# Post-norm projections of the second model's layers computed with tokens on the partitions

## The chip, the cores and the metric

The kernel runs on one core of one Trainium2 chip. The metric is the device time of one execution in microseconds (us), the median over runs. Three runs of the kernel before gave 1899.44, 1899.73 and 1900.01 us.

## What is computed

Two small models, one behind the other, on 256 tokens of width 1024, in float32, with two layers each. The first has three residual steps per layer (feed-forward, a mixer of attentions, feed-forward) and norms only before each step. The second has a mixer and a feed-forward per layer, and norms on both sides of each:

```python
    merged = gates[:, :, 0] * y_a + gates[:, :, 1] * y_b + gates[:, :, 2] * y_c
    x = x + rms_norm_2(merged @ w_o, n_post_mix)
    h = rms_norm_2(x, n_pre_ffn)
    gu = h @ w_ffn_gu
    ffn = (jax.nn.silu(gu[..., :D_FF_2]) * gu[..., D_FF_2:]) @ w_ffn_down
    return x + rms_norm_2(ffn, n_post_ffn)
```

The change is about the closing norms, `n_post_mix` and `n_post_ffn`: a projection (`w_o` or `w_ffn_down`), the mean square of its result per token, the root, the gain, the sum into the residual, and the start of the next step, which reads it.

## The kernel before, in words

The program is a list of ten stages (`STAGES`, built by `program_parts`, L167): f1, mix, f2 twice, then mix2, ff2, mix2, ff2, numbered 0 to 9. Every weight matrix is cut into parts of at most 2048 columns per partition. The parts pass through a ring of three buffers: SyncE (SP) loads part i into `raw`, ScalarE (ACT) rounds it into `w_hi` (`split_hi`, L324), VectorE (DVE) puts the rest into `w_lo` (`split_lo`, L333), and TensorE (PE) multiplies with both. `split_hi(i)` waits until part i-3 has been used (`part_used`), and each engine does its instructions in the order in which they are written. Activations are split in the same way, into `x_hl` (high and low), and a product is three matrix products: high by high, high by low, low by high.

The residual `h` lies with channels on the partitions: eight chunks of 128 channels by 256 tokens. In the feed-forward (`ffn`, L651 on PE) the weights are the stationary operand, and a row of 512 moving columns is high and low of one chunk for all 256 tokens. In the mixer the activations are stationary, one token tile of 128 tokens at a time, and the weights move.

The closing norms of stages 6, 7 and 8, which the change touches, go like this before it. The projection leaves channels on the partitions, so that a sum over channels runs across partitions. ACT squares each chunk and multiplies it by the gain (`post_gain`, L1237), DVE adds the squares up (`add_square`, L1703), PE sums over partitions with a column of ones (`closing_sum`, L593), DVE takes the mean (L1733 or L1735), GpSimd (POOL) the root (L2343), PE spreads the root over all partitions (`to_rows`, L609), DVE multiplies eight chunks by it (L1744) and adds them to `h` (L1750), ACT makes the high part of the next stage's input (L1232) and DVE the low part (L1700). Products of the next stage start as soon as the first chunk is there, and its first two parts are gone through chunk by chunk (L531/L532 in a feed-forward, `project_by_chunk`, L753, in a mixer). During the norm PE does 16 products of zeros (`warm_up`, L579).

Stage 9, the last, already has its down projection with tokens on the partitions (`down_rows`, L621 on PE; `row_square`, L1249 on ACT; `last_rows`, L1781 on DVE): hidden activations stationary, weights moving in rows of 512, one accumulator bank per token tile and half of the channels. There the sum over channels is the accumulator that comes with ACT's square.

Of the kernel before, what the change touches and what calls it, by code (L numbers as in the profile page):

```python
# [8 lines left out]
F32 = mybir.dt.float32  # L9
# [157 lines left out]
def program_parts():  # L167
# [28 lines left out]
H_BEFORE = [KC * r - 3 * sum(t == "mix2" for t, _, _ in STAGES[:r]) + 3 * sum(t == "ff2" for t, _, _ in STAGES[:r]) for r in range(len(STAGES))]  # L196

CHUNKWISE = [s > 0 and STAGES[s - 1][0] in ("mix2", "ff2") for s in range(len(STAGES))]
CHUNKS = [sum({"mix": 7, "mix2": 6}.get(t, 4) for t, _, _ in STAGES[:s]) for s in range(len(STAGES))]
SQUARES = [KC + KC * s + KC * POSTS_BEFORE[s] for s in range(len(STAGES))]  # L200
# [13 lines left out]
def build(nc, w, out):  # L214

    with ExitStack() as ctx:
# [61 lines left out]
        gained_ready, sets_clear = sem("gained_ready"), sem("sets_clear")  # L278
# [62 lines left out]
        def wait_chunk(engine, s, c):  # L341
# [7 lines left out]
            elif tag == "mix2":  # L349
                if c % 4 == 3:  # L350
                    engine.wait_ge(part_used, i0 + len(MIX2) + 2 + c // 4 + 1)
                else:
                    engine.wait_ge(chunk_done, CHUNKS[s] + 3 * (c // 4) + c % 4 + 1)
# [12 lines left out]
        def down_row_bank(m, t):  # L366
            return (6, 2)[m] + t
# [20 lines left out]
        gained = region(11264, (KC, SEQ))  # L388
        squares = rows.rearrange("p t (c n) -> p (t c) n", n=SEQ)
# [183 lines left out]
        def _(pe):  # L573
# [19 lines left out]
            def closing_sum(bank, s):  # L593

                pe.wait_ge(acc_ready, due("acc_ready"))
                for t in range(TT):
                    nc.tensor.matmul(ps[:, bank, t:t + 1], acc[:, t * P:(t + 1) * P], ones_col[:, 0:1], start=t == 0,
                                     stop=False, skip_group_check=True)
                warm_up(1)
                pe.wait_ge(sq_ready, SQUARES[s] + KC)  # L600
                for t in range(TT):
                    m = nc.tensor.matmul(ps[:, bank, t:t + 1], squares[:, KC - 1, t * P:(t + 1) * P], ones_col[:, 0:1], start=False,
                                         stop=True, skip_group_check=True)
                m.then_inc(sum_done, 1)
# [16 lines left out]
            def down_rows(i0, h0):  # L621
# [4 lines left out]
                def products(x, t):  # L626
# [4 lines left out]
                    for k in range(kc):  # L631
                        a = (hid_hl[:, k0 + k, v, t * P:(t + 1) * P] for v in range(2))
                        mm = matmul3(ps[:, down_row_bank(m, t), :], *a, hi[:, k, :], lo[:, k, :], k0 + k == 0, k0 + k == FF - 1)
                    return mm

                pe.wait_ge(hrows_ready, 4)
# [9 lines left out]
                for t in range(TT):  # L646
                    for x in (len(k_parts) - 2, len(k_parts) - 1):
                        mm = products(x, t)
                    mm.then_inc(token_done, 1)

            def ffn(s, i0, post_norm):  # L651
                x0 = due("xlo_ready", KC) - KC
                u0 = due("up_free", 2 * STEPS) - 2 * STEPS
                h0 = due("hidlo_ready", STEPS) - STEPS
                stats_at = 1 if i0 and not CHUNKWISE[s] else 2
                if CHUNKWISE[s]:
                    part_ready(i0 + 1)
                    for c in range(KC):
                        pe.wait_ge(xlo_ready, x0 + c + 1)
                        for p in range(2):  # L660
                            hi, lo = view(w_hi, i0 + p), view(w_lo, i0 + p)
                            for f in range(2):
# [1800 lines left out]
```

## Time and profile before

| | |
|---|---|
| median of three runs | 1899.73 us |
| the profiled execution's own time | 1899.96 us |
| its span, first to last instruction | 1897.8 us |
| PE busy | 1884.5 us (99%) |
| PE weight loads busy | 1639.1 us (86%) |
| DVE busy | 1340.7 us (71%) |
| ACT busy | 967.5 us (51%) |
| mean granted PE clock | 0.998 of full |
| DMA | 172 GB/s over the span |

Busy times are of instructions and overlap: a PE that streams, and one that does zeros, are both busy. So the page tells which engine bounds the kernel, and the timeline must tell what the time between two stages consists of. Matmuls overlap too: what one costs in a stream is the distance between two starts, not the length printed.

### The profile page before, as it was taken

The page shows a single profiled execution, that of the slowest core. Times are in us where ns is not written, and L with a number is a line of the kernel's source. Part 1 is how long each engine was busy: PE and PEld are TensorE (multiplying, and loading weights), DVE is VectorE, ACT ScalarE, POOL GpSimd, SP SyncE. Part 2 cuts the span into 40 slices and gives each one's busy share as a digit, 9 for nine tenths or more (in the row PEclk, how much of TensorE's full clock was granted, in tenths as well). Part 3 has the DMA queues.
Part 4 walks back from the last instruction along what each step waited for, and adds up shares of the span by engine and source line. Part 5 has one row for each costly group of instructions (what it writes and reads, how often), then busy time and mean ns, then how long its engine had stood idle before and what let it go on. Part 6 is the DMA issues. An engine that isn't in the chain of part 4 may idle for free.

```text
span 1897.8 us, 26159 instructions
## 1 busy us (share of the span) xinstructions
PE 1884.5 (99%) x10937; PEld 1639.1 (86%) x10940; DVE 1340.7 (71%) x1485; ACT 967.5 (51%) x1216; POOL 161.5 (9%) x158
## 2 busy tenths in 40 slices
PE   9999999999999999999999999999999999999998
PEld 7888879888888888898888888888888888888887
DVE  7877687787687777868776555569765654568764
ACT  5444656544444446665434665455444665455442
POOL 0000522100000006121000200000000110000000
PEclk9999999999999999999999999999999999999999
DMA  7554543455555555334554443445545343445452
GB/s 289 205 185 177 189 153 104 150 200 184 187 196 186 189 182 178 134 112 178 192 190 167 165 171 133 164 169 189 188 173 187 136 174 135 158 178 180 186 176 112
DMA packets 47491, 327.28 MB, mean 172 GB/s; under 512 B 5520, under 2 KB 5520, under 8 KB 11536
## 3 DMA queue, kind: packets, MB, share of 16 engines
q1 hardware_dynamic: 46512, 323.25, 47.0%
q10 hardware_dynamic: 864, 2.38, 0.3%
q8 instruction: 86, 1.41, 0.3%
q14 instruction: 29, 0.24, 0.0%
HBM read 324.56 MB, written 1.05 MB: 172 GB/s over the span
## 4 chain that ended last, share of the span: by engine, by line
PE 97%; DVE 1%; ACT 1%; issue 0%; DMA 0%; POOL 0%; DVEq 0%; POOLq 0%; ACTq 0%
PE ps L537 34%; PE ps L544 18%; PE ps L525 10%; PE ps L527 10%; PE ps L526 10%; PE ps L865 2%; PE ps L531 1%; PE ps L831 1%; PE ps L820 1%; PE ps L822 1%; PE ps L821 1%; PE ps L854 1%; PE ps L582 1%; PE ps L532 1%; PE ps L741 1%
## 5 line engine op out<-in xcount | busy, mean ns | idle before, releaser
L331 ACT CAST w_hi<-raw 128x2048 fp32r<-128x2048 f32 (+4 forms) x314 | 580.1, 1849 | 574.0 <-PE ps L527 193.7
L338 DVE TENSOR_TENSOR w_lo<-raw,w_hi 128x2048 fp32r<-128x2048 f32 (+4 forms) x314 | 700.1, 2231 | 237.8 <-ACT w_hi L331 235.1
L537 PE MATMUL ps<-x_hl,w_hi 128*128 128x512 f32 x1968 | 459.3, 390 | 0.0
L537 PEld LDWEIGHTS ps<-x_hl,w_hi 128*128 128x128 f32 x1968 | 365.2, 188 | 73.2
L525 PE MATMUL ps<-w_hi,x_hl 128*128 128x512 f32 (+3 forms) x672 | 262.5, 391 | 0.0
L527 PE MATMUL ps<-w_hi,x_hl 128*128 128x512 f32 (+3 forms) x672 | 254.3, 378 | 0.0
L526 PE MATMUL ps<-w_lo,x_hl 128*128 128x512 f32 (+3 forms) x672 | 253.6, 377 | 0.0
L544 PEld LDWEIGHTS ps<-x_hl,w_lo 128*128 128x128 f32 x1968 | 243.6, 192 | 5.5 <-DVE w_lo L338 1.4
L544 PE MATMUL ps<-x_hl,w_lo 128*128 128x256 f32 x1968 | 246.8, 283 | 0.8 <-DVE w_lo L338 0.8
L1816 DVE TENSOR_REDUCE ffn_tmp<-ps 128x512 f32<-128x1024 f32 x132 | 161.2, 1223 | 100.3 <-PE ps L544 50.2
L537 PE MATMUL ps<-hid_hl,w_hi 128*128 128x512 f32 x836 | 196.4, 390 | 0.0
L537 PEld LDWEIGHTS ps<-hid_hl,w_hi 128*128 128x128 f32 x836 | 154.9, 188 | 30.8
L2343 POOL TENSOR_TENSOR stat<-stat,const 128x2 f32<-128x2 f32 (+1 forms) x15 | 25.3, 1686 | 1441.4 <-DVE stat L1717 816.5
L525 PEld LDWEIGHTS ps<-w_hi,x_hl 128*128 128x128 f32 x672 | 126.5, 188 | 23.4 <-issue 2.8
L527 PEld LDWEIGHTS ps<-w_hi,x_hl 128*128 128x128 f32 x672 | 126.3, 188 | 23.6
L526 PEld LDWEIGHTS ps<-w_lo,x_hl 128*128 128x128 f32 x672 | 126.7, 189 | 19.9
L544 PEld LDWEIGHTS ps<-hid_hl,w_lo 128*128 128x128 f32 x836 | 105.2, 191 | 2.9
L544 PE MATMUL ps<-hid_hl,w_lo 128*128 128x256 f32 x836 | 106.1, 283 | 0.0
L1232 ACT ACTIVATE x_hl<-h,gains 128x256 fp32r<-128x256 f32 x80 | 39.0, 506 | 94.5 <-DVE h L1899 81.7
L1273 ACT ACTIVATE ffn_tmp<-ffn_tmp 128x512 f32<-128x512 f32 x66 | 41.8, 633 | 72.8 <-DVE ffn_tmp L1822 72.5
L1276 ACT CAST hid_hl<-ffn_tmp 128x512 fp32r<-128x512 f32 x66 | 41.1, 622 | 26.9 <-DVE ffn_tmp L1827 25.9
L531 PE MATMUL ps<-x_hl,w_hi 128*128 128x512 f32 x144 | 51.7, 402 | 0.0
(288 smaller groups left out, 2204.3 us busy)
## 6 DMA issues: line engine op xcount, KB each, us to landing
raw<-in_parts SPq DMA_DIRECT2D x278, 1024.0 KB, 4.8
raw<-in_parts SPq DMA_DIRECT2D x20, 768.0 KB, 4.2
raw<-in_parts SPq DMA_DIRECT2D x4, 928.0 KB, 4.5
raw<-in_parts SPq DMA_DIRECT2D x4, 864.0 KB, 4.4
raw<-in_parts SPq DMA_DIRECT2D x6, 512.0 KB, 3.7
raw<-in_parts SPq DMA_DIRECT2D x4, 576.0 KB, 3.6
const<-in_const ACTq DMA_DIRECT2D x1, 1093.0 KB, 5.1
h<-in_x_t SPq DMA_DIRECT2D x1, 1024.0 KB, 7.6
```

The source lines that it names most:

```text
L331: nc.scalar.copy(w_hi[:, i % RING, 0:n_of(i)], raw[:, i % RING, 0:n_of(i)]).then_inc(high_ready, 1)
L338: nc.vector.tensor_tensor(w_lo[:, s, 0:n], raw[:, s, 0:n], w_hi[:, s, 0:n].bitcast(F32), ALU.subtract).then_inc(low_ready, 1)
L525: nc.tensor.matmul(out_, a_hi, b_hi, start=start, stop=False, skip_group_check=True)
L526: nc.tensor.matmul(out_, a_hi, b_lo, start=False, stop=False, skip_group_check=True)
L527: return nc.tensor.matmul(out_, a_lo, b_hi, start=False, stop=stop, skip_group_check=True)
L531: nc.tensor.matmul(ps[:, bank, :], w_h, hl.rearrange("p x n -> p (x n)"), start=start, stop=False, skip_group_check=True)
L537: m = nc.tensor.matmul(ps[:, bank, :], w_h(c), hl(c).rearrange("p x n -> p (x n)"), start=start and c == 0, stop=stop and c == kc - 1, ski ...
L544: m = nc.tensor.matmul(ps[:, bank, 0:SEQ], w_l(c), hl(c)[:, 0, :], start=start and c == 0, stop=stop and c == kc - 1, skip_group_check=True)
L1232: nc.scalar.activation(x_hi(c), h[:, c, :], ACT.Copy, scale=gains[:, s, c:c + 1]).then_inc(xhi_ready, 1)
L1273: nc.scalar.activation(g_tmp, g_tmp, ACT.Silu).then_inc(silu_ready, 1)
L1276: nc.scalar.copy(hid_hl[:, p - 1:p + 1, 0, :], u_tmp.rearrange("p (f n) -> p f n", f=2)).then_inc(hidhi_ready, 1)
L1816: return nc.vector.tensor_reduce(dst.rearrange("p (f n) -> p f n", f=2), ps[:, b:b + 2, :].rearrange("p b (x n) -> p b n x", x=2), AX_X, A ...
```

## The change

The closing projections of stages 6, 7 and 8 get tokens on the partitions, as in stage 9. For the down projection of stage 7 that also changes how its weights are cut (`ffn_parts(..., True)`): twelve parts either way. `closing_sum`, `post_gain`, `after_post`, `post_norm` and `project_by_chunk` go away. The products of the first token tile (t0) are brought to an end before those of the second (t1), and t0's norm, with `scale_rows` on ACT, PE's transposes back (`rows_turn`) and the sums into `h` (`add_rows` on DVE), stands among t1's products. `h` and `x_hl` are then written in halves of 128 tokens by instructions of 128 by 128.

The core of the diff:

```diff
-        parts += ffn_parts("w_ffn_gu_2", 0, "w_ffn_gu_2", F, "w_ffn_down_2", l, l == DEPTH - 1)
+        parts += ffn_parts("w_ffn_gu_2", 0, "w_ffn_gu_2", F, "w_ffn_down_2", l, True)
...
+            def rows_turn(t, m, used=False):
+                pe.wait_ge(rows_scaled, due("rows_scaled"))
+                for c in range(4 * m, 4 * m + 4):
+                    tr = nc.tensor.transpose(ps[:, 2 * t + m, (c % 4) * P:(c % 4 + 1) * P], y_rows[:, t, c * P:(c + 1) * P], ident)
+                    if used and c == 4 * m:
+                        tr.then_inc(part_used, 1)
+                tr.then_inc(rows_turned, 1)
...
                 for t in range(TT):
-                    for x in (len(k_parts) - 2, len(k_parts) - 1):
-                        mm = products(x, t)
-                    mm.then_inc(token_done, 1)
+                    products(len(k_parts) - 2, t)
+                    if t == 1 and s < LAST:
+                        rows_turn(0, 0, True)
+                    products(len(k_parts) - 1, t).then_inc(token_done, 1)
+                if s < LAST:
+                    rows_turn(0, 1, True)
...
+                    if FROM_ROWS[s] and m == 0:
+                        rows_turn(1, 0)
+                        rows_turn(1, 1)
...
-                project_out(k, WO2, 3, read=(gained_ready, KC * POSTS_BEFORE[s]), x=merged_x)
-                closing_sum(STATS_MIX, s)
-                warm_up(5)
-                pe.wait_ge(gained_ready, KC * POSTS_BEFORE[s] + KC)
-                pe.wait_ge(root_ready, due("root_ready"))
-                to_rows(POST_ROW, post)
-                warm_up(10)
...
+                out_rows_of(2, 0, range(4), 11).then_inc(token_done, 1)
+                part_ready(k + 3)
+                out_rows_of(3, 0, range(4)).then_inc(token_done, 1)
+                out_rows_of(2, 1, range(4)).then_inc(token_done, 1)
+                rows_turn(0, 0, True)
+                out_rows_of(3, 1, range(2))
+                rows_turn(0, 1)
+                out_rows_of(3, 1, range(2, 4)).then_inc(token_done, 1)
+                warm_up(8, row_bank(s, 0, 0))
+                rows_turn(1, 0, True)
+                rows_turn(1, 1)
```

On ACT (feed-forward, then mixer) and on DVE (`add_rows`):

```diff
+                    split_hi(act, after)
+                    row_done()
+                    row_square(s, 1, 0)
+                    scale_rows(s, 0)
+                    for c in range(4):
+                        if c == 2:
+                            row_done()
+                            row_square(s, 1, 1)
+                        next_x_half(s + 1, 0, c, h0 + c + 1)
+                    split_hi(act, after + 1)
+                    scale_rows(s, 1)
+                    for c in range(4):
+                        next_x_half(s + 1, 1, c, h0 + KC + c + 1)
+                    for t in range(TT):
+                        for c in range(4, KC):
+                            next_x_half(s + 1, t, c, h0 + KC * t + c + 1)
+                    for c in range(KC):
+                        square(h[:, c, :], c)
+                    split_hi(act, after + 2)
...
+                for c in range(KC):
+                    if c == 5:
+                        row_done()
+                        row_square(s, 1, 1)
+                    next_x_half(s + 1, 0, c, h0 + c + 1)
+                scale_rows(s, 1)
...
+                for c in range(4 * m, 4 * m + 4):
+                    nc.vector.scalar_tensor_tensor(h[:, c, half], ps[:, 2 * t + m, (c % 4) * P:(c % 4 + 1) * P], gains[:, POST_GAIN[s], c:c + 1],
+                                                   h[:, c, half], ALU.mult, ALU.add).then_inc(h_ready, 1)
```

How the instructions move, at three places.

**PE, from the last products of `w_o` to the first of the feed-forward, before.** L820 to L822 are the products, L597 and L602 the sum over partitions, L609 the spreading, L582 the zeros.

```order
L822 MATMUL ps<-y_hl,w_lo 128x256
L597 MATMUL ps<-const,arena 128x1 x2
L582 MATMUL ps<-unsel 128x512
L602 MATMUL ps<-const,rows 128x1 x2
L582 MATMUL ps<-unsel 128x512 x5
L609 MATMUL ps<-const,stat 128x128 x2
L582 MATMUL ps<-unsel 128x512 x10
L531 MATMUL ps<-x_hl,w_hi 128x512
```

**The same place now.** L528 to L530 are the products with rows of 512, L600 the transposes, L585 the zeros.

```order
L530 MATMUL ps<-w_hi,y_hl 128x512
L600 MATMUL ps<-const,arena 128x128 [waits rows_scaled]
L600 MATMUL ps<-const,arena 128x128 x3
...
L530 MATMUL ps<-w_hi,y_hl 128x512
L585 MATMUL ps<-unsel 128x512 x8
L600 MATMUL ps<-const,arena 128x128 [waits rows_scaled]
L600 MATMUL ps<-const,arena 128x128 x3
L600 MATMUL ps<-const,arena 128x128 [waits rows_scaled]
L600 MATMUL ps<-const,arena 128x128 x3
L534 MATMUL ps<-x_hl,w_hi 128x512 [waits xlo_ready,low_ready]
```

Half of the sixteen transposes stand among the products, half behind the zeros; all zeros come before the first transpose of t1.

**DVE at the same place now.** L1763 is `add_rows`, L1770 the low half of the next input, L1754 (`row_root`) t1's mean square.

```order
L1763 SCALAR_TENSOR_TENSOR h<-ps,gains,h 128x128 x3
L1770 SCALAR_TENSOR_TENSOR x_hl<-h,gains,x_hl 128x128 [waits xhi_ready] x4
L1754 SCALAR_TENSOR_TENSOR stat<-stat 128x1 [waits outsq_ready]
L1763 SCALAR_TENSOR_TENSOR h<-ps,gains,h 128x128 [waits rows_turned]
```

t1's mean square stands behind the last low halves of t0.

**ACT, from stage 7 to the mixer of stage 8, before.** L1238 is the gain, L331 a part's rounding, L1232 the next input, L1235 a square of `h`.

```order
L1238 ACTIVATE arena<-ps,gains 128x256 x2
L331 CAST w_hi<-raw 128x1728 [waits part_used,raw_in1]
L1232 ACTIVATE x_hl<-h,gains 128x256 [waits h_ready] x2
L1235 ACTIVATE rows<-h 128x256 x2
```

**The same place now.**

```order
L1240 ACTIVATE x_hl<-h,gains 128x128 [waits h_ready] x2
L338 CAST w_hi<-raw 128x2048 [waits part_used,raw_in0]
L1246 ACTIVATE arena<-ps,stat 128x512 [waits root_ready]
L1246 ACTIVATE arena<-ps,stat 128x512
L1240 ACTIVATE x_hl<-h,gains 128x128 [waits h_ready] x12
L1234 ACTIVATE rows<-h 128x256 x8
L338 CAST w_hi<-raw 128x1728 [waits part_used,raw_in1]
```

The rounding of the next stage's second part has moved behind t0's first inputs, and that of its third part (1728 columns) behind all inputs and squares.

## Rows read from the trace of the kernel before

**Rows 1.** The chain that ended last, shares of the span by engine.

```profile
PE 97%; DVE 1%; ACT 1%; issue 0%; DMA 0%; POOL 0%; DVEq 0%; POOLq 0%; ACTq 0%
```

**Rows 2.** Stretch around stages 6 and 7: from:to, us, busy (count) by engine, PEclk, DMA, GB/s.

```profile
1260.00:1280.00 20.00, 19.50 (x143) 16.90 (x144) 10.73 (x18) 12.81 (x23) 0.70 (x1) 1.00 0.44 159
```

**Rows 3.** Timeline of PE, w_o into stage 7: start us, length us, instruction, shape, count.

```profile
1248.63 0.28 PE L820 MATMUL ps<-x_hl,w_hi 128*128 128x256 f32 x1
...
1251.51 1.04 PE L741 MATMUL ps<-const,rows 128*128 128x128 f32 x8
1252.30 0.36 PE L820 MATMUL ps<-x_hl,w_hi 128*128 128x256 f32 x1
...
1272.41 0.28 PE L822 MATMUL ps<-y_hl,w_lo 128*128 128x256 f32 x1
...
1275.90 2.32 PE L582 MATMUL ps<-unsel 128*128 128x512 bf16 x10
1278.19 0.47 PE L531 MATMUL ps<-x_hl,w_hi 128*128 128x512 f32 x1
...
1289.74 3.85 PE L537 MATMUL ps<-x_hl,w_hi 128*128 128x512 f32 x16
```

**Rows 4.** Timeline of stage 9: a product of 512 columns, then t0's square, accumulator and root.

```profile
1887.54 0.39 PE L526 MATMUL ps<-w_lo,hid_hl 128*128 128x512 f32 x1
1887.77 0.39 PE L527 MATMUL ps<-w_hi,hid_hl 128*128 128x512 f32 x1
...
1888.19 0.60 ACT L1251 ACTIVATE arena<-ps 128x512 f32<-128x512 f32 x1 [8.42 <-PE ps L527]
1888.69 0.19 ACT L1251 ACTIVATION_READ_ACCUMULATOR arena<-ps 128x1 f32 x1
...
1889.15 0.55 POOL L2343 TENSOR_TENSOR stat<-stat,const 128x1 f32<-128x1 f32 x1 [162.98 <-DVE stat L1797]
```

**Rows 5.** Groups by form, ACT and DVE: shapes, count, busy us, mean ns, idle before.

```profile
L331 ACT CAST w_hi<-raw 128x2048 fp32r<-128x2048 f32 x276 | 526.2, 1907 | 509.0 <-PE ps L527 177.5 <-PE ps L544 161.8 <-PE ps L537 130.3
L1232 ACT ACTIVATE x_hl<-h,gains 128x256 fp32r<-128x256 f32 x80 | 39.0, 506 | 94.5 <-DVE h L1899 81.7 <-DVE h L1750 12.1
L1235 ACT ACTIVATE rows<-h 128x256 f32<-128x256 f32 x80 | 30.2, 402 | 0.0
L1284 ACT ACTIVATE neg_ident<-const 128x128 bf16<-128x128 f32 x1 | 0.3, 294 | 0.0
L1700 DVE SCALAR_TENSOR_TENSOR x_hl<-h,gains,x_hl 128x256 fp32r<-128x256 f32 x80 | 39.6, 511 | 10.4 <-ACT x_hl L1232 10.4
L338 DVE TENSOR_TENSOR w_lo<-raw,w_hi 128x1728 fp32r<-128x1728 f32 x4 | 7.8, 1952 | 0.0
L2158 DVE SCALAR_TENSOR_TENSOR arena<-arena,ps 128x128 f32<-128x128 f32 x8 | 2.4, 345 | 0.1
```

**Rows 6.** Timeline, stage 7's down projection into the mixer of stage 8.

```profile
1401.92 1.30 PE L537 MATMUL ps<-hid_hl,w_hi 128*128 128x512 f32 x5
...
1463.47 0.28 PE L527 MATMUL ps<-hid_hl,w_lo 128*128 128x256 f32 x1
...
1464.79 1.64 ACT L331 CAST w_hi<-raw 128x1728 fp32r<-128x1728 f32 x1
...
1468.70 0.47 PE L525 MATMUL ps<-w_hi,x_hl 128*128 128x512 f32 x1
...
1483.28 0.70 POOL L2343 TENSOR_TENSOR stat<-stat,const 128x2 f32<-128x2 f32 x1 [17.48 <-DVE stat L1717]
1484.07 1.27 ACT L1518 ACTIVATE arena<-ps,stat 128x512 f32<-128x512 f32 x2 [6.30 <-POOL stat L2343]
1485.39 0.87 PE L741 MATMUL ps<-const,arena 128*128 128x128 f32 x6
```

**Rows 7.** The start of the kernel: ten products of zeros after a gap, and the granted clock.

```profile
7.21 4.01 PE L582 MATMUL ps<-unsel 128*128 128x512 bf16 x10 [2.11 <-ACT w_hi L315]
...
7.50:8.00 0.50, 0.50 (x3) 0.14 (x2) 0.50 (x2) 0.50 (x2) 0.00 (x0) 0.69 1.02 426
...
11.00:11.50 0.50, 0.50 (x4) 0.43 (x3) 0.50 (x2) 0.50 (x2) 0.00 (x0) 0.90 1.08 459
```

More of the change, by code:

```diff
@@ L195, with half_place @@
 POSTS_BEFORE = [sum(t in ("mix2", "ff2") for t, _, _ in STAGES[:r]) for r in range(len(STAGES))]
[L196 to L200, printed above, removed]
+H_BEFORE = [KC * r for r in range(len(STAGES))]
+FROM_ROWS = [s > 0 and STAGES[s - 1][0] in ("mix2", "ff2") for s in range(len(STAGES))]
+CHUNKS = [sum({"mix": 7, "mix2": 0, "ff2": 0}.get(t, 4) for t, _, _ in STAGES[:s]) for s in range(len(STAGES))]
+SQUARES = [KC + KC * s for s in range(len(STAGES))]
+def half_place(s, t, c):
+    if STAGES[s - 1][0] == "mix2":
+        return KC * t + c + 1
+    return KC * (c // 4) + 4 * t + c % 4 + 1
 class Due:
@@ L780, in project @@
                                 pe.wait_ge(*ready(o + c))
+                            if t == 1 and c0 == 0 and late is not None:
+                                pe.wait_ge(*late(o + c))
                             a_hi, a_lo = x(o + c)
@@ L803, in project_out @@
                 hi, lo = view(w_hi, i), view(w_lo, i)
-                last = m == 3 or parts is WO2 and m == 2
+                last = m == 3
                 for n in range(n_all // P):
@@ L1169, in mixer2 @@
                 for m, (name, _, _, k, kc, g, last) in enumerate(MIX2):
-                    free = ready = None
+                    free = ready = late = None
                     if g >= 2 and k == 0:
@@ L1185, in mixer2 @@
                         x, ready = whole_x, lambda c: (S["tlo_ready"], 8 + c // 2)
[L1186 to L1189 removed]
+                    project(i0 + m, pair_bank(g), kc, o, k == 0, last, free, ready, x, lambda: within_part(m), late)
                     after_part(m)
@@ new lines, in mixer2 @@
+                part_ready(k + 3)
[8 more added lines that the diff above has]
+                rows_turn(1, 1)
+                for t in range(TT):
+                    due("root_ready")
@@ L1766, in post_norm, with next_x_lo_half, sum_squares @@
+            def next_x_lo_half(s, t, m):
+                half = slice(t * P, (t + 1) * P)
+                for c in range(4 * m, 4 * m + 4):
+                    dve.wait_ge(xhi_ready, due("xhi_ready"))
+                    nc.vector.scalar_tensor_tensor(x_lo(c)[:, half], h[:, c, half], gains[:, s, c:c + 1], x_hi(c)[:, half].bitcast(F32), ALU.mult,
+                                                   ALU.subtract).then_inc(xlo_ready, 1)
+            def sum_squares():
                 for c in range(KC):
@@ L1795, in last_rows @@
[L1795 to L1804 removed]
+                            row_mean(s, t, t + 1, True)
@@ new lines, in down_in_rows @@
+                            if s == LAST:
+                                gain_rows(0, t)
+                if s == LAST:
+                    for t in range(TT):
+                        row_root(s, t, TT + t + 1)
+                        step(gain_rows(1, t))
+                        dve.wait_ge(root_ready, due("root_ready", 0))
+                        for m in range(2):
+                            r = out_rows[:, t, 512 * m:512 * m + 512]
+                            nc.vector.scalar_tensor_tensor(r, r, post[:, t:t + 1], h_rows[:, t, 512 * m:512 * m + 512], ALU.mult,
+                                                           ALU.add).then_inc(out_ready, 1)
+                    return
@@ L1852, in ffn @@
                 scaled_gate(0)
-                if s and not CHUNKWISE[s]:
+                if s and not FROM_ROWS[s]:
                     split_lo(dve, i0 + 4)
```

342 lines of the change are left out of this document (141 added, 201 removed).

## The prediction

> **What bounds the kernel now.** I read the chain of waits first: 97% of it is PE [rows 1]. So time changes only where PE streams fewer columns, or where it has nothing useful to stream. The windows are all but full there too: PE is busy 19.50 of 20 us around the end of stage 6, at the full clock [rows 2]. That hides what the timeline shows: the last product of `w_o` starts at 1272.41, the first of stage 7 at 1278.19, and between them PE does sums, spreading and products of zeros [rows 3]. Products of 256 columns follow each other by 0.12 us, so the gap is 1278.19 - 1272.53 = 5.66 us. From stage 7 to 8 it is 1468.70 - 1463.59 = 5.11 [rows 6]. Stage 8 to 9 repeats the first. These three gaps, 16.4 us, and the form of the products are what the change can reach. The groups by form and stage 9, which already works by token tiles, give the prices [rows 4, 5].
>
> **Products.** Rows of 512 columns follow each other by 0.227 us [rows 4]; two of 256 cost 0.24. `w_o` now has 8 x 8 x 3 = 192 products of 256: 23.04 us. By rows it has 2 x 2 x 8 x 3 = 96 of 512: 21.8. That saves 1.27 us, twice. Stage 7's down projection takes 1463.59 - 1401.92 = 61.67 [rows 6] and becomes 22 x 2 x 2 x 3 = 264 of 512: 59.85. That saves 1.8.
>
> **Transposes.** Each closing adds 16, eight of them among products. The trace has eight in 1252.30 - 1251.51 = 0.79 us [rows 3], 0.10 each, so 0.8 us of PE time beside the 0.8 in the gap, three times. The Trainium skill, "TensorE: Matmul & The Clock Gate", Part 4: PE-mode transpose, has about 275 ns for one in a kernel's context; if all 48 queued at that, they would take 13.2 us instead of 4.8, and the row speaks against it: that is one's length, and they overlap.
>
> **Small instructions.** `h`, the high and the low parts go from 256 to 128 columns each. DVE: a scalar_tensor_tensor of 128 columns takes 0.345 us, one of 256 takes 0.511 [rows 5]. Starts of like instructions lie some 0.08 to 0.1 closer than their length, so I take 0.27 apart. The ends are 0.22 (half a step of 256) and 0.38 (nearly what 256 costs); I stay at the row of the same shape. ACT: a rounding with the gain takes 0.506 for 256 columns, a copy of 128 takes 0.294 [rows 5]. I take 0.40 long and 0.30 apart, ends as for DVE. A rule speaks against smaller pieces: the Trainium skill, "VectorE: DVE Perf Modes", The TRN2 errata, says each instruction pays a fixed latency whatever its size and wants tiles of 512 or more; its formula gives ScalarE 352 cycles, 0.29 us, for 128 columns, which would leave the sum below as it is. The trace agrees so far: half the columns cost well over half the time.
>
> **w_o into a feed-forward, twice.** t0 first. Its square, accumulator, mean and root take 1.7 us from its last product's slot (1888.00 to 1889.70 in stage 9 [rows 4]), the first scaling 0.7 more: ready at 2.5, wanted by PE at 2.72 (12 products of t1). So t0's norm hides, with 0.2 to spare. Then t1, in us from the end of its last product:
> - result seen and square with accumulator: 0.2 + 0.7 = 0.9;
> - DVE isn't free: the mean square stands behind t0's last low halves, whose high halves of chunks 5 to 7 stand behind this square on ACT (each 0.30): 2.1;
> - mean 0.16, hand-over 0.08, root 0.55: 2.9;
> - scaling 0.69, then four transposes with their drain, 0.57: 4.3;
> - four sums into `h` by DVE at 0.27 before its first low half: 5.4; the low half 0.35: 5.8.
>
> The gap is 5.8 us instead of 5.66: the norm is one tile instead of two but has more steps in line. After it, the first part is fed by pairs of 0.7 us a chunk, slower than DVE's 0.54 (a sum and a low part), so it doesn't stall. The second part's rounding (1.9 us on ACT [rows 5]) ends 1.4 us before PE wants it. In all, from the first product of `w_o` to the end of the second part: before, 1289.74 - 1248.63 = 41.11 [rows 3]. Then: products 21.8, transposes within it 0.8 + 0.8, gap 5.8, two parts of 5.6: 40.2. **-0.9 us, twice.** With DVE and ACT at their ends -1.4 or +1.2 each.
>
> **Stage 7 into the mixer.** Here only t0 is needed to start. t1's last product ends at 0. PE turns t0's second half (0.4), and the four chunks of t0 that are ready cover 2.7. t1: DVE's mean square comes only after four low halves and four sums of t0, at 3.0; root at 3.7, scaling seen at 4.4. PE has been idle from 3.1 to 4.4, turns t1 (1.0), and waits until 6.5 for the first low half. t1's first chunks last until 9.3. DVE then splits the second part (2.2) before t0's upper half, 0.6 lost; eight chunk steps of 0.68 end at 15.3. Now the third part. ACT rounds it behind the last high half (12.1), eight squares of 0.31 (14.6; 0.402 long [rows 5]) and its own 1.64 [rows 6]: 16.2. DVE's 1.9 [rows 5] gives 18.2. **PE stands 2.9 us there**, where before ACT rounded that part at 1464.79, before the inputs [rows 6]. Then the sum of squares: as before, PE waits behind that part for root and scaling to turn the mixer's first rows (1483.28, 1484.07, 1485.39 [rows 6]), but these follow DVE's split of the fourth part: some 1.6 us of waiting instead of 0.3. The turn starts 24.8 us after t1's end. From the start of the down projection: 59.85 + 0.4 (one turn among the products) + 24.8 = 85.1; before, 1485.39 - 1401.92 = 83.5 [rows 6]. **+1.6 us**, ends +0.8 and +4.1. Behind that both do the same.
>
> **Sum of the work**: 2 x (-0.9) + 1.6 = -0.2; with the ends -2.0 and +6.5.
>
> **The clock.** Before, zeros fill every gap. Now PE has holes: behind eight zeros (1.7 us) idle 1.95, transposes, idle 1.1; in stage 8 idle 1.3, transposes, idle 1.1, and the 2.9. The one hole in the trace is 2.1 us, before the second set of zeros at the start; half a us later the clock fell to half (0.69 in that half us) and was full again within 11.00 to 11.50 (0.90 [rows 7]). Ten products of zeros then took 4.01 instead of 2.32 [rows 3]: 1.7 us for one fall. Part of a fall lies in waiting, so I take 1.1 to 1.7 for a fall in front of a feed-forward and less before the mixer. It need not happen: the transposes divide the holes. I take two falls in three: **+2.0 us**, ends 0 and +5.
>
> **Forecast.** -0.2 + 2.0 = +1.8 on the profiled execution's 1899.96 (span 1897.8 and 2.2 around it): 1901.8; the median of the runs stands 0.2 lower, so **1901.6 us**. A change of less than 0.2%, 3.8 us, is about what a measurement of this kernel can't tell from none.
>
> **Rivals.**
> - *The clock holds.* For it: transposes keep the array at work, and zeros come just before. Against: rows 7. Only the sum remains: -0.2, 1899.5. Chance 0.23.
> - *Small instructions at their upper end, slower by over 0.2%.* Where DVE and ACT take 0.38 per half, the gap before a feed-forward is 7.6 instead of 5.8 and the mixer's third part comes 2.4 later. t0's scaling also runs late among t1's products (0.2 us to spare), and each such wait delays t1 as well. Sum +6.5, with longer holes and so a fall almost surely, +1.5: 1907.7. It decides from about 0.33 on. For it: four engines hand over ten times in line. Against: the row of 0.345 [rows 5]. Chance 0.20.
> - *Faster.* The lower end (-2.0), the clock held, and DVE's wait behind t0's low halves gone because ACT has done them before t1's last product: that gives 1.2 back at each feed-forward: -4.4, 1895.3. For it: DVE is idle there otherwise. Against: chunk 5 is put behind the square by the order of the program. Chance 0.10.
> - *The change hides nothing*: t0's norm, as priced, ends as PE wants it; if it took 2 us more (ACT or DVE still in a part's splitting, 1.9 and 2.2 us), PE would stand among t1's products: 2 us at each closing on top of +1.8, 1907.5. Against: the last split before it ends over 1 us earlier. Chance 0.05.
>
> The forecast itself has the remaining 0.42; its own range is 1899.5 to 1904.
>
> **Numbers.** Of the forecast's chance a quarter (0.10) lies above 1903.5, as do the second and last rivals (0.20 and 0.05): slower 0.35. Faster by over 0.2% needs the third rival: 0.10. Within 0.2%: the rest of the forecast and the held clock, 0.55. The range from 1896.5 to 1906.5 leaves out 0.08 below and 0.12 above.
>
> **What would show it.** Right: 96 products by `w_o` at 0.227 apart; a gap of about 5.8 us before the feed-forwards, with DVE's mean square behind t0's last low halves; PE standing 1.1 to 1.5 us on both sides of t1's transposes; in stage 8 a wait of about 3 us for `w_lo` of the third part; stretches of half clock behind the holes. Wrong: half instructions at other prices than 0.27 and 0.30, a gap under 4 us, a third part that isn't waited for, or a clock of 1.00 in every stretch.

## The result, and the profile after

The changed kernel takes 1901.93 us in the median, against 1899.72 for the kernel before on the same chip: a ratio of 1.0013, interval 1.0007 to 1.0019. That is 2.2 us more, against 1.9 forecast. One of its twenty runs (7588.06 us), and one of the eleven of the first experiment below (3135.74), was disturbed: the medians given count them (without them they are 1901.13 and 1900.76), and the ratios, the counts of runs and the ranges leave them out. The profiled execution took 1900.76 us, its span is 1898.3.

The 19 runs do not lie evenly: ten between 1900.4 and 1901.1, at a mean granted clock of about 0.999, six between 1902.7 and 1903.7 at about 0.997, three between 1904.6 and 1905.5 at 0.995 to 0.996. No run lies between 1901.13 and 1902.74. So the median of 1901.93 is the middle of an empty stretch, where no run was; the nineteen have a median of 1901.13 (+1.4) and a mean of 1902.16 (+2.45 against the other kernel's mean of 1899.71). The kernel before spread over 1.3 us in all. So the change did two things: it moved the fastest group by +1.0 (its median is 1900.68), and it spread the runs.

Busy times from the page, then the stretch that answers to [rows 2] (from:to, us, busy by PE, PEld, DVE, ACT, POOL, PEclk, DMA, GB/s):

```profile
PE 1875.5 (99%) x10594; PEld 1620.3 (85%) x10596; DVE 1330.3 (70%) x1512; ACT 969.3 (51%) x1228; POOL 162.7 (9%) x161
...
PE 95%; DVE 2%; ACT 1%; DMA 0%; issue 0%; POOL 0%; DVEq 0%; POOLq 0%; SPq 0%; ACTq 0%
```

```profile
1260.00:1280.00 20.00, 17.22 (x86) 13.23 (x86) 11.09 (x37) 12.39 (x30) 1.10 (x2) 1.00 0.29 104
```

PE has lost 9 us of busy time, and the chain of waits now runs over DVE and ACT in 3% instead of 2%. In the stretch it is busy 17.22 instead of 19.50 us, at the full clock in this execution.

**In front of a feed-forward.** The timeline of PE, `w_o` of stage 6 into stage 7, answers to [rows 3]:

```profile
1248.06 0.39 PE L528 MATMUL ps<-w_hi,x_hl 128*128 128x512 f32 x1
...
1250.80 1.09 PE L725 MATMUL ps<-const,rows 128*128 128x128 f32 x8
...
1268.09 0.60 PE L600 MATMUL ps<-const,arena 128*128 128x128 f32 x4
...
1269.90 0.60 PE L600 MATMUL ps<-const,arena 128*128 128x128 f32 x4
...
1271.50 0.40 PE L530 MATMUL ps<-w_hi,y_hl 128*128 128x512 f32 x1
1271.96 1.67 PE L585 MATMUL ps<-unsel 128*128 128x512 bf16 x7
1275.36 1.24 PE L600 MATMUL ps<-const,arena 128*128 128x128 f32 x8 [1.72 <-ACT arena L1246]
1277.58 0.47 PE L534 MATMUL ps<-x_hl,w_hi 128*128 128x512 f32 x1 [0.99 <-DVE x_hl L1770]
...
1286.87 3.40 PE L547 MATMUL ps<-x_hl,w_lo 128*128 128x256 f32 x27
```

L600 are the transposes back, L585 the zeros (the trace has seven of the eight). Neither transpose of t0 carries a wait: its norm is hidden. From the last product's slot (1271.73) to the first of stage 7 is 5.85 us. The second part ends 16 low products of 0.12 behind 1286.87, at 1288.79: 40.73 us after the start of `w_o`. What DVE does in that gap:

```profile
1272.94 0.94 DVE L1770 SCALAR_TENSOR_TENSOR x_hl<-h,gains,x_hl 128x128 fp32r<-128x128 f32 x3 [0.56 <-ACT x_hl L1240]
1273.79 0.15 DVE L1754 SCALAR_TENSOR_TENSOR stat<-stat 128x1 f32<-128x1 f32 x1
1276.05 1.13 DVE L1763 SCALAR_TENSOR_TENSOR h<-ps,gains,h 128x128 f32<-128x128 f32 x4 [2.10 <-PE ps L600]
1277.09 1.13 DVE L1770 SCALAR_TENSOR_TENSOR x_hl<-h,gains,x_hl 128x128 fp32r<-128x128 f32 x4
```

The mean square of t1 (L1754) does stand behind t0's last three low halves, 2.06 us after the last product.

**Stage 7 into the mixer** answers to [rows 6]; ACT and DVE first, then PE:

```profile
1471.93 1.28 ACT L1240 ACTIVATE x_hl<-h,gains 128x128 fp32r<-128x128 f32 x4 [2.89 <-DVE h L1763]
1473.12 2.55 ACT L1234 ACTIVATE rows<-h 128x256 f32<-128x256 f32 x8
1475.58 3.15 ACT L338 CAST w_hi<-raw 128x1728 fp32r<-128x1728 f32 x2
...
1477.22 1.96 DVE L345 TENSOR_TENSOR w_lo<-raw,w_hi 128x1728 fp32r<-128x1728 f32 x1 [3.51 <-ACT w_hi L338]
```

```profile
1400.81 0.40 PE L528 MATMUL ps<-w_hi,hid_hl 128*128 128x512 f32 x1
...
1465.51 1.24 PE L600 MATMUL ps<-const,arena 128*128 128x128 f32 x8 [0.98 <-ACT arena L1246]
1467.64 0.50 PE L528 MATMUL ps<-w_hi,x_hl 128*128 128x512 f32 x1 [0.90 <-DVE x_hl L1770]
...
1479.24 0.47 PE L528 MATMUL ps<-w_hi,x_hl 128*128 128x432 f32 x1 [2.56 <-DVE w_lo L345]
...
1486.34 0.87 PE L725 MATMUL ps<-const,arena 128*128 128x128 f32 x6
```

PE stands 2.56 us for the third part's low half, whose rounding waits on ACT behind the squares, after ACT had been idle for 2.89 us. In this execution the clock falls behind that hole. Stretches with PE alone (from:to, us, busy, PEclk, DMA, GB/s):

```profile
1479.00:1480.00 1.00, 0.76 (x3) 0.87 0.00 0
1480.00:1482.00 2.00, 2.00 (x7) 0.50 0.93 246
1484.00:1486.00 2.00, 2.00 (x12) 1.00 0.70 217
```

Full clock until the product behind the hole, then half (0.50, the level of 1.2 GHz), full again by 1484.

Three stretches hold the change (us; "full clock": from a run without a fall there):

| | before | forecast | after |
|---|---|---|---|
| `w_o` to the second part's end, stage 6 to 7 | 41.11 | 40.2 | 40.73 |
| the same, stage 8 to 9 | 41.12 | 40.2 | 40.84 |
| stage 7's down projection to the turn of the mixer's rows | 83.47 | 85.1 | 85.53; 85.01 at full clock |

At the full clock that makes -0.38 - 0.28 + 1.54 = +0.9, close to the +1.0 of the fastest group. What lifts the mean of the nineteen by another 1.5 us (1902.16 against 1900.68) is the spread.

The two profiled executions lie only 0.8 us apart, though the three stretches as profiled (85.53) make +1.4. The difference comes from the kernel's start: the ten zeros of [rows 7], which took 4.01 us at a fallen clock, take 2.33 here, and `w_o` of stage 6 starts 0.57 us earlier, at 1248.06 instead of 1248.63. The change touches nothing there.

```profile
7.14 2.33 PE L585 MATMUL ps<-unsel 128*128 128x512 bf16 x10 [1.59 <-ACT w_hi L322]
```

### The profile page after: what moved, and what is told of

Same layout as the page of the kernel before. It is cut to its first block, busy times and chain, and to the rows that moved or that the text cites. A ratio compares the mean times of both kernels' runs of the same rounds, so it can differ in the third digit from the quotient of the medians.

```text
span 1898.3 us, 25490 instructions
## 1 busy us (share of the span) xinstructions
PE 1875.5 (99%) x10594; PEld 1620.3 (85%) x10596; DVE 1330.3 (70%) x1512; ACT 969.3 (51%) x1228; POOL 162.7 (9%) x161
## 4 chain that ended last, share of the span: by engine, by line
PE 95%; DVE 2%; ACT 1%; DMA 0%; issue 0%; POOL 0%; DVEq 0%; POOLq 0%; SPq 0%; ACTq 0%
PE ps L540 32%; PE ps L547 17%; PE ps L528 12%; PE ps L530 11%; PE ps L529 11%; PE ps L838 2%; PE ps L804 1%; PE ps L534 1%; PE ps L827 1%; DVE w_lo L345 1%; PE ps L725 1%; PE ps L793 1%; PE ps L795 1%; PE ps L794 1%; PE ps L535 1%; PE ps L854 0%
## 5 line engine op out<-in xcount | busy, mean ns | idle before, releaser
L540 PE MATMUL ps<-x_hl,w_hi 128*128 128x512 f32 x2000 | 466.6, 390 | 0.0
L528 PE MATMUL ps<-w_hi,x_hl 128*128 128x512 f32 (+3 forms) x704 | 275.9, 392 | 3.8 <-DVE w_lo L345 2.6
L530 PE MATMUL ps<-w_hi,x_hl 128*128 128x512 f32 (+3 forms) x704 | 267.4, 380 | 0.0
L529 PE MATMUL ps<-w_lo,x_hl 128*128 128x512 f32 (+3 forms) x704 | 266.7, 379 | 0.0
L540 PE MATMUL ps<-hid_hl,w_hi 128*128 128x512 f32 x704 | 165.5, 390 | 0.0
L528 PEld LDWEIGHTS ps<-w_hi,x_hl 128*128 128x128 f32 x704 | 133.0, 189 | 28.5 <-DVE w_lo L345 4.0
L530 PEld LDWEIGHTS ps<-w_hi,x_hl 128*128 128x128 f32 x704 | 132.8, 189 | 24.9
L540 PEld LDWEIGHTS ps<-hid_hl,w_hi 128*128 128x128 f32 x704 | 130.4, 188 | 25.9
L547 PEld LDWEIGHTS ps<-hid_hl,w_lo 128*128 128x128 f32 x704 | 88.7, 191 | 2.5
L547 PE MATMUL ps<-hid_hl,w_lo 128*128 128x256 f32 x704 | 89.5, 283 | 0.0
L528 PE MATMUL ps<-w_hi,hid_hl 128*128 128x512 f32 x176 | 68.6, 390 | 0.0
L529 PE MATMUL ps<-w_lo,hid_hl 128*128 128x512 f32 x176 | 68.5, 389 | 0.0
```

The costliest lines, as they stand in the source:

```text
L528: nc.tensor.matmul(out_, a_hi, b_hi, start=start, stop=False, skip_group_check=True)
L529: nc.tensor.matmul(out_, a_hi, b_lo, start=False, stop=False, skip_group_check=True)
L530: return nc.tensor.matmul(out_, a_lo, b_hi, start=False, stop=stop, skip_group_check=True)
L540: m = nc.tensor.matmul(ps[:, bank, :], w_h(c), hl(c).rearrange("p x n -> p (x n)"), start=start and c == 0, stop=stop and c == kc - 1, ski ...
L547: m = nc.tensor.matmul(ps[:, bank, 0:SEQ], w_l(c), hl(c)[:, 0, :], start=start and c == 0, stop=stop and c == kc - 1, skip_group_check=True)
```

## The experiments

A fall is a stretch in which the granted clock drops from full to half. My theory: +0.9 us of work and waits, which is -0.7 in front of the feed-forwards and +1.5 in PE's wait for the mixer's third part; and on top of it falls of the clock in the holes in front of the feed-forwards, which come in some runs and make the groups. The rivals: the spread has another cause; the small instructions are the cost; t0's norm hides nothing.

### Zeros in the holes, all of them and by place

```diff
-                warm_up(8, row_bank(s, 0, 0))
+                warm_up(16, row_bank(s, 0, 0))
                 rows_turn(1, 0, True)
                 rows_turn(1, 1)
+                warm_up(5, row_bank(s, 0, 0))
...
                     if FROM_ROWS[s] and m == 0:
+                        warm_up(4, 6)
                         rows_turn(1, 0)
                         rows_turn(1, 1)
+                        warm_up(4, 6)
...
+                    if FROM_ROWS[s] and m == 2:
+                        warm_up(12, 6)
```

The first run has both pieces, the second only the upper one (in front of the feed-forwards), the third only the lower one (stage 8).

> The changed kernel, with products of zeros put into the holes that PE has in the three closings: eight more behind t1's last product and five more behind its transposes in front of the two feed-forwards, eight around t1's transposes and twelve before the third part at the start of stage 8. If falls of the clock in these holes are what makes many runs of the changed kernel longer by steps of some 2.3 us, then all runs lie near the fastest group, 1900.4 to 1901.2, the median falls from 1901.9 to about 1900.7, the profile shows no stretch of half clock at 1479.7 to 1483.1, and the runs' mean granted clocks are all alike. If the steps come from something else (transfers, the start of the kernel), the groups stay and the median stays at 1901.9 or more. If the length of the chain of small instructions is the cost, the zeros change nothing, or, where they last longer than the hole, add up to 0.5 us each.

> Only the zeros in front of the two feed-forwards. If the falls that come and go between runs lie in front of the feed-forwards (the profiled run has none there, but one in stage 8 in full), the groups at 1902.7 to 1905.5 disappear and the median is 1900.6 to 1901.2; the fall at 1480 in stage 8 stays. If they lie in stage 8, or at the kernel's start, the groups stay and the median is 1901.9.

> Only the zeros at the start of stage 8, around t1's transposes and before the third part. If the clock's fall at 1479.7 to 1483.1 costs time, the turn of the mixer's first rows comes earlier than 1486.3; at most by what of the fall does not lie in waiting, 0 to 1 us, since these rows wait for the chain over DVE, GpSimd and ScalarE. The groups of runs stay if the falls in front of the feed-forwards make them. If all falls are here, the groups go with this one alone.

Measured: 1900.82, 1900.96 and 1902.79 us. With zeros in front of the feed-forwards all runs, ten and eleven, lie between 1900.3 and 1901.5: the groups are gone. With zeros in stage 8 alone they stay: five runs at 1900.2 to 1901.0, five at 1902.8 to 1904.0, one at 1905.5. So the spread comes from the holes in front of the feed-forwards. The fall in stage 8 costs 0.5 us up to the turn in the changed kernel's profile (85.53 against 85.01 us with zeros there, where PE waits 1.17 us in front of the turn instead of not at all); 1900.82 against 1900.96 us is too close to show it.

One part of the second expectation missed: I had the fall at 1480 stay, and in that run's profile it isn't there. The clock fell one hole earlier, behind t1's transposes (columns of [rows 2]):

```profile
1468.00:1470.00 2.00, 1.86 (x4) 1.49 (x5) 2.00 (x5) 1.53 (x6) 0.00 (x0) 0.50 0.00 0
1480.00:1482.00 2.00, 2.00 (x12) 1.91 (x11) 1.93 (x4) 0.00 (x0) 0.00 (x0) 1.00 0.64 160
```

PE then waits 1.66 us for the third part instead of 2.56, and the turn comes at 85.01 us all the same: there the wait takes the whole fall, and it costs nothing. The profiles without zeros and with the mean square first, further down, show the same (waits of 1.64 and 1.63 us, turns at 85.00).

The profiled execution of the third run (1902.97 us) has a fall at both places in front of the feed-forwards. Its stretches with PE alone:

```profile
1278.00:1280.00 2.00, 2.00 (x8) 0.50 0.00 0
1709.00:1710.00 1.00, 1.00 (x5) 0.50 0.00 0
```

From the first product of a feed-forward to the end of its first part: 7.25 and 6.95 us, against 5.62 and 5.72 in the changed kernel's profile; 1.6 and 1.2 us for the two, together about the distance between this run's first two groups (medians 1900.34 and 1903.07, 2.7 us). They came together here. What decides in which run they come stays open.

### No zeros

```diff
-                warm_up(8, row_bank(s, 0, 0))
```

> The eight products of zeros before t1's transposes are taken out of the two closings in front of feed-forwards, so that the hole on their left grows from 1.7 to 3.4 us. If holes bring the clock down, each of the two falls comes in nearly every run: the profile shows a half-clock stretch behind both gaps, and the median rises by 2 to 4.6 us, to 1904 to 1906.5. If the clock does not mind holes of this length, nothing changes: 1901.9.

Measured: 1905.59 us, all seven runs between 1903.9 and 1905.9. Stretches behind the first closing, with the columns of [rows 2]:

```profile
1272.00:1275.00 3.00, 0.07 (x1) 0.00 (x0) 1.54 (x7) 1.77 (x6) 0.55 (x1) 1.00 0.01 3
1275.00:1276.00 1.00, 0.47 (x2) 0.48 (x3) 0.00 (x0) 1.00 (x2) 0.00 (x0) 0.72 0.00 0
1276.00:1282.00 6.00, 5.28 (x20) 4.34 (x19) 4.26 (x16) 4.18 (x10) 0.00 (x0) 0.50 0.00 0
```

Without zeros the clock is at half already during the transposes, for over 6 us. No run lies near the fastest group, so I take it that the falls came every time; only one of the seven has its trace. The eight products of zeros that the change has there turn a loss of some 4.9 us (1905.59 against 1900.68) in all runs into one of 2.3 to 4.6 in nine of nineteen.

### The third part rounded early

```diff
                         for c in range(4, KC):
                             next_x_half(s + 1, t, c, h0 + KC * t + c + 1)
+                        if t == 0:
+                            split_hi(act, after + 2)
                     for c in range(KC):
                         square(h[:, c, :], c)
-                    split_hi(act, after + 2)
```

> In stage 7's closing ScalarE rounds the mixer's third part before t1's upper high halves and the eight squares, in an idle stretch of 2.9 us, instead of behind them. If my step on the third part is right (PE stands 2.7 us for its low part, and the mixer's rows wait behind that), PE does not stand there, and the turn of the mixer's first rows comes 2 to 4 us earlier than 85.5 us after the start of the down projection; the kernel gets 2 to 4 us faster than the changed one, 1898 to 1899.5 in the median. If the turn is held by the sum of squares and the root instead, the stall only moves and the time stays within 0.7 us of 1901.9.

Measured: 1897.52 us, half a us under the range that I expected, with seven of eleven runs at 1897.0 to 1897.8 (the others, up to 1901.9, at the lower clocks of the falls). The timeline of ACT, then of PE:

```profile
1469.06 1.63 ACT L338 CAST w_hi<-raw 128x1728 fp32r<-128x1728 f32 x1
1472.03 1.28 ACT L1240 ACTIVATE x_hl<-h,gains 128x128 fp32r<-128x128 f32 x4 [1.34 <-DVE h L1764]
1473.22 2.55 ACT L1234 ACTIVATE rows<-h 128x256 f32<-128x256 f32 x8
```

```profile
1482.63 0.87 PE L725 MATMUL ps<-const,arena 128*128 128x128 f32 x6 [0.71 <-ACT arena L1529]
```

The rounding fits into the idle stretch, PE does not stand for the third part, and the turn comes 81.71 us after the start of the down projection instead of 85.01 at the full clock: -3.3 us, and 1.8 less than in the kernel before. So the +1.5 hung on this one place in ACT's order.

### The mean square first

```diff
                 add_rows(s, 0, 1)
-                next_x_lo_half(s + 1, 0, 1)
                 row_root(s, 1, 4)
+                next_x_lo_half(s + 1, 0, 1)
```

> In the closings in front of the feed-forwards VectorE takes t1's mean square before t0's last three low halves instead of behind them. If the norm of t1 is the chain that PE waits for, the gap there gets 0.9 to 1.2 us shorter, twice: -2 us and fewer falls, 1899 to 1900. If PE waits for the low halves just as much (t0's chunks 5 to 7 come later), nothing or little is won: within 0.5 us.

Measured: 1898.76 us, 0.2 under the range. The gap is 4.76 us instead of 5.85, at both feed-forwards: -1.09 each, and PE doesn't miss the low halves. Only one of eleven runs was slower than 1899.7; it is the profiled one, 1901.76, and its stretches, with the same columns, show what one fall looks like:

```profile
1277.00:1278.00 1.00, 0.92 (x4) 0.81 (x5) 1.00 (x5) 0.21 (x1) 0.00 (x0) 0.74 0.00 0
1278.00:1280.00 2.00, 2.00 (x8) 1.71 (x7) 1.80 (x7) 1.98 (x5) 0.00 (x0) 0.50 0.00 0
1280.00:1281.00 1.00, 1.00 (x5) 0.90 (x4) 0.00 (x0) 1.00 (x2) 0.00 (x0) 0.55 0.00 0
1281.00:1282.00 1.00, 1.00 (x7) 0.87 (x6) 0.89 (x1) 1.00 (x2) 0.00 (x0) 1.00 0.00 0
```

Its first parts take 7.24 and 7.20 us: 1.5 to 1.6 each.

### t0 turned late

```diff
+                out_rows_of(3, 1, range(4)).then_inc(token_done, 1)
                 rows_turn(0, 0, True)
-                out_rows_of(3, 1, range(2))
                 rows_turn(0, 1)
-                out_rows_of(3, 1, range(2, 4)).then_inc(token_done, 1)
```

> In the closings in front of the feed-forwards PE turns t0 back behind all of t1's products, not among them. If the change hides t0's norm under t1's products, this gives back part of what it hides: DVE's sums of t0 begin 3 us later and stand in front of t1's mean square, so the gap grows by 1.5 to 3 us at each of the two, +3 to +6 in all, 1905 to 1908. If t0's norm hides nothing (the rival), the time stays at 1901.9.

Measured: 1910.34 us, 2.3 above the end of what I expected. The gap is 9.23 us, of which 0.92 are the two turns that left the products: 9.23 - 5.85 - 0.92 = 2.5 each, within 1.5 to 3. The whole stretch says the same: from the first product of `y_hl` to the first of the feed-forward it is 20.11 us (1260.18 to 1280.29) instead of 17.66 (1259.92 to 1277.58).

```profile
1271.06 1.04 PE L600 MATMUL ps<-const,arena 128*128 128x128 f32 x8
1280.29 0.76 PE L534 MATMUL ps<-x_hl,w_hi 128*128 128x512 f32 x1 [0.94 <-DVE x_hl L1769]
```

The rest is the clock. With a longer hole PE idles 4.24 us behind the zeros, all five runs have a mean granted clock of 0.993 to 0.996, and the first parts take 8.26 and 7.50 us instead of 5.7 (at the second feed-forward the gap itself is 0.46 longer too). I had priced the chain and forgotten what its hole does to the clock.

### All three, and four more steps

The three edits together, with eleven and five products of zeros in front of the feed-forwards and four on each side of t1's transposes in stage 8:

> The third part rounded early, the mean square first, and zeros in the holes (eleven and five in front of the feed-forwards, eight around t1's transposes in stage 8). If the three effects are independent: 1900.6 at a steady clock, less 2 to 4, less 2: 1894.6 to 1896.6, faster than both kernels by about 0.2%. If they share one bound (the same wait ends both), it lands at 1898 to 1899.

Measured: 1895.08 us (1894.3 to 1895.7), ratio to the kernel before 0.9977, interval 0.9968 to 0.9985. So the effects add up: 1900.8 with the holes filled, less 3.3 and twice 1.09, is 1895.3.

Then t1's root early in stage 7, with one product of zeros instead of four in front of t1's transposes there:

```diff
-                    split_hi(act, after + 1)
                     scale_rows(s, 1)
+                    split_hi(act, after + 1)
...
-                next_x_lo_half(s + 1, 0, 0)
-                add_rows(s, 0, 1)
+                next_x_lo_half(s + 1, 0, 0, 0, 2)
                 row_root(s, 1, 4)
+                next_x_lo_half(s + 1, 0, 0, 2)
+                add_rows(s, 0, 1)
```

> On top of the kernel with all three edits (1895.1): in stage 7's closing VectorE takes t1's mean square behind t0's first two low halves, and ScalarE scales t1 before it rounds the mixer's second part; three fewer zeros before t1's transposes. If t1's norm is what PE waits for at the start of stage 8 (t1's transposes now at 1465.20, the last product of t0's ready chunks at 1463.81), the transposes and all that follows come some 1.1 us earlier: 1894.0. If the mixer's second or fourth part becomes late instead (its rounding and its low part come later on both engines), it gives that back: 1895.1 or more.

Measured: 1894.13. From the down projection to the turn 80.84 instead of 81.71: -0.87, most of the 1.1. (The two kernels ran on different chips; the medians of the kernel before differ by 0.07 us.) Then two that missed:

```diff
-                if FROM_ROWS[s]:
-                    split_lo(dve, i0 + 3)
                 token_roots(STATS_MIX)
+                if FROM_ROWS[s]:
+                    split_lo(dve, i0 + 3)
```

> As the one before, and in stage 8 VectorE splits the mixer's fourth part behind the means for the mixer's first rows instead of in front of them. PE waits 0.72 us for these rows now, and the mean stood 1.3 us behind that split: 0.7 us less, 1893.3, if nothing else is late; 1894.0 if the sums of PE (which stand behind the third part) hold the mean just as long.

```diff
-                add_rows(s, 1, 0)
-                next_x_lo_half(s + 1, 1, 0)
+                add_and_split(s, 1, 0)
```

> As the one before, and in all three closings VectorE turns to t1's first low half after two sums into the residual instead of four. In front of the feed-forwards the first low half then waits for ScalarE's high half and comes 0.3 us earlier, twice: 0.6 us less, 1892.7. If PE is fed too thinly behind it (a sum and a low part by 0.52 us a chunk, against 0.7 us of products), no gain.

Measured: 1895.75 and 1896.52 us, slower by 1.6 and by another 0.8. For the first, the timelines of POOL and DVE with t1's root early, and then with the fourth part late:

```profile
1478.24 1.95 DVE L345 TENSOR_TENSOR w_lo<-raw,w_hi 128x1728 fp32r<-128x1728 f32 x1
...
1480.29 0.16 DVE L1741 TENSOR_SCALAR stat<-ps 128x2 f32<-128x2 f32 x1
...
1480.53 0.70 POOL L2372 TENSOR_TENSOR stat<-stat,const 128x2 f32<-128x2 f32 x1 [16.69 <-DVE stat L1741]
```

```profile
1478.63 0.16 DVE L1741 TENSOR_SCALAR stat<-ps 128x2 f32<-128x2 f32 x1
1478.71 1.95 DVE L345 TENSOR_TENSOR w_lo<-raw,w_hi 128x1728 fp32r<-128x1728 f32 x1
...
1478.87 2.35 POOL L2372 TENSOR_TENSOR stat<-stat,const 128x2 f32<-128x2 f32 x1 [16.23 <-DVE stat L1741]
```

The means came 0.46 us earlier, counted from the start of the down projection, but DVE began to split 0.16 us before POOL began the root, and the root lasted until 0.56 us after the split's end: 2.35 us instead of 0.70. PE waited 1.88 us for it. For the second, in stage 7 the first low half comes no earlier (its high half waits on ACT behind the rounding of the second part), the split of that part starts 0.7 us later, and PE waits 1.13 us instead of 0.37 for the low half behind it: 82.77 us up to the turn instead of 82.03. In this execution the clock falls there as well (0.80 over 1480 to 1485), in the other it does not, behind the same 1.88 us of waiting. In front of the feed-forwards the same edit does gain: the gap is 4.54 instead of 4.76.

The last run keeps what worked, with t1's first low half after two sums in front of the feed-forwards only, and tests the reading of the root:

```diff
+                token_roots(STATS_MIX)
+                n = due("root_ready")
                 if FROM_ROWS[s]:
+                    dve.wait_ge(root_ready, n)
                     split_lo(dve, i0 + 3)
```

> The kernel of 1894.1 (t1's root early in stage 7) with two more edits. In stage 8 VectorE splits the fourth part only when GpSimd's root is done. If that split, started 0.2 us before the root, is what made the root last 2.35 us instead of 0.70, the root is back at 0.70, ScalarE's scaling follows, and PE goes on with the fourth part some 0.4 us earlier than at 1894.1. If the root was long for another reason, it stays at 2.3 and the kernel lies at 1895.7. And the closings in front of the feed-forwards (not the one of stage 7) take t1's first low half after two sums: 0.22 less each, read from the profile before. Together 1893.3.

```profile
1478.23 0.70 POOL L2381 TENSOR_TENSOR stat<-stat,const 128x2 f32<-128x2 f32 x1 [16.20 <-DVE stat L1741]
...
1478.96 1.96 DVE L345 TENSOR_TENSOR w_lo<-raw,w_hi 128x1728 fp32r<-128x1728 f32 x1 [0.81 <-POOL stat L2381]
```

Measured: 1893.22 us (1892.9 to 1893.4, five runs), ratio to the kernel before 0.9965, interval 0.9951 to 0.9978. The root is back at 0.70. This version is 6.7 us faster than the kernel before on the same chip, and 7.5 faster than the fastest group of the change (1900.68, on another chip).

## Why the prediction was right, point by point

1901.6 us was forecast, and 1901.93 measured. That it agrees to 0.3 is luck: no run of the changed kernel lies within 0.4 us of the forecast, the nineteen have their median at 1901.13 and their mean at 1902.16, and two errors cancel in part: the sum of the work was 1.1 us too low, the clock's term 0.5 to 1.6 too high. The direction, and most of the steps, were right for the reasons given.

- **Prices of small instructions.** Right. Four of 128 columns take DVE 1.13 us, 0.26 apart (0.27 taken), and ACT 1.28, 0.29 apart (0.30 taken). The rival of small instructions at their upper end needed 0.33 and is out.
- **Transposes.** 0.10 was taken. Their mean length is 279 ns, near the 275 that the Trainium skill has ("TensorE: Matmul & The Clock Gate", Part 4: PE-mode transpose), but four take 0.60 us in all, so they are 0.11 apart. A turn among products takes 0.46 (two turns and 12 products of 0.227 between 1268.09 and 1271.73), not 0.40, since the stream pays for entering and leaving it. Some 0.1 us more at each closing, from a row that showed only a longer group.
- **The gap in front of a feed-forward.** 5.8 forecast, 5.85 measured at both, with the mean square behind t0's low halves as said, and t0's norm hidden. The run with the late turn shows that the hiding is worth 2.5 us at each, so the rival that it hides nothing is out.
- **w_o to the second part's end.** Here a step failed: -0.9 twice was forecast, -0.38 and -0.28 measured. Some 0.3 of that are the turns, the mixer's own eight included (0.97 in the stream instead of 0.79). Another 0.2 is a slip: 21.8, 1.6, 5.8 and two times 5.6 make 40.4, and the text says 40.2. The first part took 5.72 us between stages 8 and 9 and 5.62 between 6 and 7, which I can't place.
- **Stage 7 into the mixer.** The turn was forecast 85.1 us after the start; 85.01 at the full clock. PE standing for the third part: 2.9 forecast, 2.7 in starts (2.56 idle). The early rounding takes this away, and the wait for the mixer's rows doesn't grow in its place (0.71 us), which shows the cause. The wait for these rows behind the third part was forecast at 1.6 and is 1.17 at the full clock.
- **Sum of the work.** -0.2 forecast, +0.9 measured; the whole difference is in `w_o`.
- **The clock.** Right in place and price, wrong in how it adds up. A fall in front of a feed-forward was priced at 1.1 to 1.7 us; 1.2 to 1.6 were measured. "Two in three" was meant as falls in one execution. The groups say that the two come together in nine of nineteen runs, sometimes at nearly double the price, and not at all in ten; no trace of the changed kernel shows them, those of the third and of the mean-first run show two at once. The fall in stage 8 costs half a us or nothing, since the waits for the third part and for the mixer's rows cover it. +2.0 was forecast; measured is +1.5 in the mean of the nineteen, +0.45 in their median, and +1.25 by the median that lies in the empty stretch. This made up for the sum.
- **The clock holds**, the rival at 1899.5, is refuted by the groups; with the holes filled the kernel lies at 1900.8, 1.3 us above what that rival gave for this condition, mostly the slip and the turns.
- **The signs.** Holes of 1.1 to 1.5 us on both sides of t1's transposes were forecast; they are 1.72 and 0.99 in front of the feed-forwards, 0.98 and 0.90 in stage 8. Half clock stood behind the hole in stage 8 only in the profiled execution.
- **Faster.** It named DVE's wait behind t0's low halves as worth 1.2 us at each closing; taking it away gave 1.09. It was the order of the program that decided, as said.

## What to carry to other kernels

Splitting a tile to hide half of a serial chain pays 2.5 us at each closing in front of a feed-forward here, but the other half still stands open, and a change that swaps filler work for real work makes holes. Ask at each hole what the clock does behind it, and look at every run's time, not only the profiled one: the profiled execution here had no fall where the cost lay. When an instruction is written behind others "because it is needed later", look for the idle stretch before it: two moved lines gave 3.3 and 2.2 us. Neither changes a count of instructions; only the order on ACT and DVE.

## What the runs showed of the hardware that I had not expected

- **A VectorE split locks GpSimd out.** POOL's root on two columns takes 0.70 us, and 2.35 when DVE's split of 1.95 us, with both inputs in SBUF, has just begun. Holding the split back by 0.81 us brought the turn from 82.03 us to 80.35, as much as the root had lost. The kernel before has the case too, in stage 7, and it could have warned me:

```profile
1294.80 2.28 DVE L338 TENSOR_TENSOR w_lo<-raw,w_hi 128x2048 fp32r<-128x2048 f32 x1
1294.97 2.67 POOL L2343 TENSOR_TENSOR stat<-stat,const 128x2 f32<-128x2 f32 x1 [19.73 <-DVE stat L1717]
```

  The Trainium skill, "SBUF — State Buffer", SBUF: two separate sides, says so: a DVE instruction with two SBUF inputs and a GpSimd one that reads SBUF exclude each other for the whole instruction. The traces agree: the root ends 0.56 us after the split in both.
- **The clock's fall depends on the run.** The same program, with the same holes, has runs without it in front of the feed-forwards and runs with it (ten and nine of nineteen, by their times and mean granted clocks of 0.999 and 0.995 to 0.997). With no zeros in the hole all seven runs lie at 0.994 to 0.996.
- **The fall can come in the hole or behind it.** In stage 8 PE was idle up to 1479.24, and the granted clock fell only behind that (0.87 over 1479 to 1480, then 0.50); without zeros in front of the feed-forward it had fallen before the idle stretch ended (0.72 over 1275 to 1276). So a full clock in the idle stretch doesn't show that a hole cost nothing; look at the products behind it.
